# ScalarE's order in the feed-forward inputs, index rotations and Relu in PSUM, the angles in front of the down projection f3_dn

## The reference, cut to what matters

```
h = concat(meta, x)                               # 16 + 256 tokens, 1024 wide
for i in range(2):                                # first model
    h = h + 0.5 * swiglu(rms_norm(h, g[0]), ...)  # f0, f2
    hn = rms_norm(h, g[1])
    h = h + (rwkv7_time_mix(hn, ...) if i == 0 else dsa_attention(hn, ...))
    h = h + 0.5 * swiglu(rms_norm(h, g[2]), ...)  # f1, f3
# swiglu: gate, up = split(h @ w_in); (silu(gate) * up) @ w_out, d_ff 2816
# dsa_attention: an index decides which keys each query sees
qi = partial_rope(qi); ki = partial_rope(ki)      # x * cos + rotated(x) * sin
rel = relu(einsum("bqhd,bkd->bqhk", qi, ki))
score = einsum("bqh,bqhk->bqk", wi, rel)          # then top_k of score
# second model, one layer: two attentions, one with apply_rope on
# ang = positions * inv_freq (cos(ang), sin(ang) computed on the chip), then
hid = square(relu(rms_norm_2(h) @ w_ff1)); h = h + hid @ w_ff2   # 4096 wide
```

## Time and profile before

| what | us |
|---|---|
| median of 3 runs (1659.41 to 1664.03) | 1660.43 |
| profiled execution, its time | 1659.63 |
| its span (first to last instruction) | 1657.8 |
| TensorE busy | 1578.5 |
| GpSimd busy | 1132.7 |
| ScalarE busy | 758.3 |
| VectorE busy | 703.4 |
| mean granted TensorE clock, share of full speed | 0.982 |

### The profile page before, as it was taken

How to read it: one execution, slowest core, us unless ns; L and a number is a source line. 1 busy time by engine, 2 the same in 40 slices (tenths; PEclk the granted TensorE clock), 3 DMA queues, 4 the chain that set the end, 5 groups by cost and what they waited for, 6 DMA issues and landing times.

```text
span 1657.8 us, 40970 instructions
## 1 busy us (share of the span) xinstructions
PE 1578.5 (95%) x16236; PEld 1499.6 (90%) x16236; DVE 703.4 (42%) x1549; ACT 758.3 (46%) x1271; POOL 1132.7 (68%) x835
## 2 busy tenths in 40 slices
PE   6999989899989999999999999999999999989998
PEld 6999989688878999999999986698999978789998
DVE  4332068664556333223331387665321455443300
ACT  5444446743324444454444443554445525545532
POOL 5777858683416777877778773187888954358895
PEclk9999999899999999999999999999999989999999
DMA  6544523310013444455445530164546522225552
GB/s 245 175 171 147 183 100 131 128 65 3 3 53 128 171 172 150 167 203 177 171 145 175 198 137 18 32 234 153 188 153 215 172 102 102 77 92 186 181 203 76
DMA packets 37910, 231.34 MB, mean 140 GB/s; under 512 B 4527, under 2 KB 6680, under 8 KB 16552
## 3 DMA queue, kind: packets, MB, share of 16 engines
q1 hardware_dynamic: 36552, 228.57, 39.2%
q10 hardware_dynamic: 1248, 1.24, 0.2%
HBM read 228.67 MB, written 2.63 MB: 140 GB/s over the span
## 4 chain that ended last, share of the span: by engine, by line
PE 86%; DVE 6%; issue 3%; ACT 2%; POOL 2%; DMA 0%; DVEq 0%; SPq 0%; ACTq 0%; POOLq 0%
PE PS L770 71%; PE PS L769 2%; POOL wlo L724 2%; PE PS L991 1%; PE PS L1368 1%; PE PS L1006 1%; PE PS L998 1%; DVE krot L2326 1%; ACT whi L2492 1%; DVE xl L1702 1%; DMA raw<-w_f_in_in 0%; PE PS L785 0%; PE PS L1030 0%; PE PS L1036 0%; PE PS L1156 0%
## 5 line engine op out<-in xcount | busy, mean ns | idle before, releaser
L724 POOL TENSOR_TENSOR wlo<-raw,whi 128x256 fp32r<-128x256 f32 (+2 forms) x759 | 1086.0, 1462 | 468.8 <-ACT whi L2492 411.8
L770 PE MATMUL PS<-xh,whi 128*128 128x272 f32 (+1 forms) x2336 | 676.5, 290 | 30.2 <-POOL wlo L724 23.9
L770 PE MATMUL PS<-xl,whi 128*128 128x272 f32 (+1 forms) x2336 | 668.6, 286 | 0.0
L770 PE MATMUL PS<-xh,wlo 128*128 128x272 f32 (+1 forms) x2336 | 668.2, 286 | 0.0
L2492 ACT ACTIVATE whi<-raw 128x1024 fp32r<-128x1024 f32 x472 | 449.6, 982 | 259.8 <-PE PS L770 223.2
L770 PEld LDWEIGHTS PS<-xh,whi 128*128 128x128 f32 x2336 | 440.9, 189 | 39.6 <-issue 26.3
L770 PEld LDWEIGHTS PS<-xl,whi 128*128 128x128 f32 x2336 | 442.1, 189 | 0.4
L770 PEld LDWEIGHTS PS<-xh,wlo 128*128 128x128 f32 x2336 | 442.4, 189 | 0.0
L770 PE MATMUL PS<-hid_h,whi 128*128 128x272 f32 (+1 forms) x960 | 274.1, 285 | 4.2 <-POOL wlo L724 4.2
L770 PE MATMUL PS<-hid_h,wlo 128*128 128x272 f32 (+1 forms) x960 | 273.8, 285 | 0.0
L770 PE MATMUL PS<-hid_l,whi 128*128 128x272 f32 (+1 forms) x960 | 272.8, 284 | 0.0
(11 more groups left out here) (381 smaller groups left out, 1624.4 us busy)
## 6 DMA issues: line engine op xcount, KB each, us to landing
raw<-w_f_in_in SPq DMA_DIRECT2D x88, 1024.0 KB, 4.8
raw<-w_f_dn_in SPq DMA_DIRECT2D x64, 704.0 KB, 4.0
raw<-w_b_ff_in SPq DMA_DIRECT2D x32, 1024.0 KB, 4.8
raw<-w_rk_k_in SPq DMA_DIRECT2D x4, 1024.0 KB, 4.9
raw<-w_rk_r_in SPq DMA_DIRECT2D x4, 1024.0 KB, 5.0
raw<-w_rk_v_in SPq DMA_DIRECT2D x4, 1024.0 KB, 4.9
raw<-w_rk_o_in SPq DMA_DIRECT2D x4, 1024.0 KB, 4.8
raw<-w_at_q_in SPq DMA_DIRECT2D x4, 1024.0 KB, 5.0
```

The costliest lines, as they stand in the source:

```text
L724: last = nc.gpsimd.tensor_tensor(wlo[U % SPL][:, piece], raw[U % RAW][:, piece], whi[U % SPL][:, piece].bitcast(F32), ALU.subtract)
L770: mm(out, a, b, start=start and n == 0, stop=stop and n == 2, **kw)
```

## The change

It has five edits, with the same work on TensorE, GpSimd and SyncE's queues.

1. ScalarE in the input projections: after the sigmoid of unit u stands `hi(u + 2)`, then `high(u - 1)`. The last four units are written out.
2. The index rotations: a product `rcos = rstd * cos` is made once. The cosine parts are then made from PSUM with `rcos`, the sine parts in PSUM, and one addition is left. `tailr` no longer marks the group as drained; the second reader of that PSUM group, which uses `rcos`, does.
3. Relu of the index products in PSUM; VectorE reads it there, and TensorE waits for VectorE's additions (`index_added`) before it uses the bank again.
4. The 18 angle instructions in one run behind f3's input projection, ahead of the first addition of `f3_dn`; the two `Sin` behind the first two chunks on ScalarE.
5. In `b_ff1` VectorE takes the norm's sum before it waits for the unit, and ScalarE does `hi(u + 2)` ahead of the squares of unit u.

```diff
-            pe.wait_ge(s_free, G0["at_tail"] + 1)
+            pe.wait_ge(s_tail, 1)
...
-                    pe.wait_ge(s_rl, n - 1)
+                    pe.wait_ge(s_ra, 2 * n - 2)
...
-                        if f == "f3" and i is None:
-                            angle_piece(u)
...
-            v.tensor_tensor(tailr[0:72, :], PS[0:72, bank(G), 0:T], rstd[0:72, 0:T], ALU.mult).then_inc(s_free, 1)
+            v.tensor_tensor(tailr[0:72, :], PS[0:72, bank(G), 0:T], rstd[0:72, 0:T], ALU.mult).then_inc(s_tail, 1)
...
+            def index_cosine(u):
+                U, G = U0["at_qi"] + u, G0["at_qi"] + u
+                dve.wait_ge(s_unit, 2 * (U + 1))
+                x, src = qiT[:, 2 * u:2 * u + 2, :], PS[:, bank(G):bank(G) + 2, 0:SEQ]
+                step.do(v.tensor_tensor(x, src, rstd[:, META:T].unsqueeze(1).broadcast_to([128, 2, SEQ]), ALU.mult))
+                v.tensor_tensor(sqq[:, 2 * u:2 * u + 2, :], src, rcos[:, META:T].unsqueeze(1).broadcast_to([128, 2, SEQ]),
+                                ALU.mult).then_inc(s_free, 1)
+
+            def index_sum(u):
+                dve.wait_ge(s_irot, u + 2)
+                ps = PS[:, 4 + 2 * u:6 + 2 * u, 0:SEQ]
+                step(v.tensor_tensor(ps, ps, cs_a[:, 1:2, META:T].broadcast_to([128, 2, SEQ]), ALU.mult))
+                v.tensor_tensor(qiT[:, 2 * u:2 * u + 2, :], sqq[:, 2 * u:2 * u + 2, :], ps, ALU.add).then_inc(s_iout, 1)
+
+            dve.wait_ge(s_dsc, 48)
+            step.do(v.tensor_tensor(rcos[:, :], rstd[:, :], cs_a[:, 0, :], ALU.mult))
+            step.sync()
+            v.tensor_tensor(rta[0:64, 0, :], PS[0:64, bank(G), 0:T], rcos[0:64, :], ALU.mult).then_inc(s_free, 1)
+            index_cosine(0)
...
+            angle_begin()
+            for n in range(2):
+                if n:
+                    dve.wait_ge(s_ang, 1)
+                angle_turns(n)
+                angle_reduced(n)
+                angle_end(n)
             residual("f3_dn", SEQ, 1, 2, 0.5, "b", VEC["norm_mix"], "b")
...
-                    dve.wait_ge(s_unit, val(2 * (U + 1), i, 8))
                     if u == 0:
                         rms("ff", SEQ)
+                    dve.wait_ge(s_unit, val(2 * (U + 1), i, 8))
...
-                        w = last_width(name, u) if u == us[-1] else UW[name]
-                        hi(U0[name] + u + 1, i, 4, w)
-                        if u == 0:
-                            root(fn, n)
                         act.wait_ge(s_gate, val(hb + u + 1, i, 4))
                         f(sig[:, u % 2, 0:n], PS[:, hbank(u), 0:n], ACT.Sigmoid).then_inc(s_sig, 1)
+                        hi(U0[name] + u + 2, i)
                         if u >= 1:
                             high(u - 1, i)
...
-                if n >= 2:
-                    act.wait_ge(s_ra, 2 * n - 2)
-                f(rel[:, n % 2, :, 0:nk], PS[:, 4 + 2 * (n % 2):6 + 2 * (n % 2), 0:nk], ACT.Relu).then_inc(s_rl, 1)
+                ps = PS[:, 4 + 2 * (n % 2):6 + 2 * (n % 2), 0:nk]
+                f(ps, ps, ACT.Relu).then_inc(s_rl, 1)
...
+            residual("f3_dn", SEQ, 1, 2, "b", "b", beside=sines)
...
-                    hi(U0["b_ff1"] + u + 1, i, 4, 2048)
-                    if u == 0:
-                        root("ff", SEQ)
+                    hi(U0["b_ff1"] + u + 2, i)
                     act.wait_ge(s_free, val(G0["b_ff1"] + u + 1, i, 4))
```

More of the change, by code:

```diff
@@ L2151, in index_scores @@
                     dve.wait_ge(s_ra, 2 * n + e + 1)
-            drain_at("at_qi", 0, qiT[:, 0:2, :], META)
-            dve.wait_ge(s_free, G + 1)
+            def index_cosine(u):
[15 more added lines that the diff above has]
+            index_cosine(0)
+            dve.wait_ge(s_free, G + 2)
             dve.wait_ge(s_irot, 1)
[L2156 to L2159, removed]
+            ps = PS[0:64, 7, 0:T]
+            step(v.tensor_tensor(ps, ps, cs_a[0:64, 1, :], ALU.mult))
+            v.tensor_tensor(kiT[0:64, :], rta[0:64, 0, :], ps, ALU.add).then_inc(s_iout, 1)
             dve.wait_ge(s_rcm, 1)
@@ L2530, in body, with residual @@
                 def body(us, i):
-                    us = list(us)
                     for u in us:
-                        w = last_width(name, u) if u == us[-1] else UW[name]
-                        hi(U0[name] + u + 1, i, 4, w)
-                        if u == 0:
-                            root(fn, n)
                         act.wait_ge(s_gate, val(hb + u + 1, i, 4))
                         f(sig[:, u % 2, 0:n], PS[:, hbank(u), 0:n], ACT.Sigmoid).then_inc(s_sig, 1)
+                        hi(U0[name] + u + 2, i)
                         if u >= 1:
                             high(u - 1, i)
-                turns(step, FC, 4, 0, body, 2)
-                hi(U0[fn + "_dn"] + 1)
+                hi(U0[name] + 1)
+                root(fn, n)
+                body(range(2), None)
+                with step.loop((FC - 6) // 4, 0) as i:
+                    body(range(2, 6), i)
+                body(range(FC - 4, FC), None)
                 high(FC - 1, None)
-            def residual(name, n, w, units, norm, split, done=0):
+            def residual(name, n, w, units, norm, split, done=0, beside=None):
                 per = 4 if w == 2 else 2
@@ L2573, in body @@
                                 after_add(j - 1, i)
+                    if beside and i is None:
+                        beside()
                 turns(step, 8 // w, per, 0, body, 1)
@@ L2831, in _, with sines @@
             swiglu_in("f3")
-            for n in range(2):
-                act.wait_ge(s_ang, n + 1)
-                f(cs_b[:, n, :], cs_b[:, n, :], ACT.Sin).then_inc(s_sin, 1)
-            residual("f3_dn", SEQ, 1, 2, "b", "b")
+            def sines():
+                for n in range(2):
+                    act.wait_ge(s_ang, n + 1)
+                    f(cs_b[:, n, :], cs_b[:, n, :], ACT.Sin).then_inc(s_sin, 1)
+            residual("f3_dn", SEQ, 1, 2, "b", "b", beside=sines)
             def latent(g):
@@ L2948, in ff1 @@
                     f(hid2_h[:, o], act2[:, u % 2, :, :].rearrange("p m n -> p (m n)"), ACT.Square).then_inc(s_hf2, 1)
+            hi(U0["b_ff1"] + 1)
+            root("ff", SEQ)
             ff1(range(4), None)
@@ L2951, in _ @@
                 ff1(range(4, 8), i)
-            for u in range(16):
+            for u in range(1, 16):
                 hi(U0["b_ff2"] + u + 1)
```

29 lines of the change are left out of this document (7 added, 22 removed).

## The result

The changed kernel takes 1652.53 us (median of 8 runs, 1649.81 to 1656.25), the kernel before 1662.66 beside it (8 runs): ratio 0.9942, interval 0.9923 to 0.9961, faster by 10.1 us in the medians and by some 9.6 by the ratio, which takes all runs. The prediction was 1664.3, +3.9. The span of the profiled execution is 1652.3, 5.5 less than before.

A forecast was written before the change was run, and what follows sets the result against it. TensorE, busy 1578.5 of 1657.8 us, was taken as the bound, so its waits and half clock count. -10.5 removed, +7.5 in f3_dn and +6.9 in the index part gave +3.9 on 1660.43: 1664.3 us, range 1652.5 to 1667.5.

The forecast's parts named there:

- I go by the first, since `rcos` meets the very same run without gaps: Index part: `rcos` is shut out until GpSimd's run ends at 954.7, TensorE waits 7.25 us: +6.9.
- rival B: Index part: `rcos` is let in after one GpSimd piece, -2.1 to -2.4 there; total 1655.1 us; chance 0.31.
- f3_dn: Its start: angles, slowed by GpSimd, stop TensorE for 5.8 us, plus 1.7 of clock: +7.5, bounds 0 and 10.5.
- C: Start of f3_dn: the angles hide there, no stall; 1656.8 us, or 1647.6 with `rcos` let in; chance 0.17.
- Rival D: Behind both new waits the clock stays at 0.50 for 5.40 us, costing 2.7 each, not 1.7; 1666.3 us; chance 0.12.
- E: Second units of the down projections: their waits stay despite the change; +4.2 over the forecast, 1668.5 us; chance 0.03.
- What the change removes: TensorE's waits for `wlo` at the down projections' second units, in f3's input projection and in `b_ff1` go: -10.5 us.
- The down starts: Second units of the down projections: `hi` ahead of the last two `hid_h` removes TensorE's waits: -4.2 us.
- f3's input projection: Without the angles there, TensorE's waits of 2.03 and 1.91 us for `wlo` go: -3.9.
- `b_ff1`: Norm's sum half a unit earlier and `hi(u + 2)` ahead of the squares remove TensorE's wait for `wlo`: -2.4 us.
- the new order costs nothing inside the loop: Input projections: `hid_h` is late by one `hi` but read only by the down projection, so no cost.
- Edits at nothing: Relu in PSUM (bounds -0.3 and +0.5) and the two `Sin` with table load on idle ScalarE: taken as 0 us.

The follow-up runs named there:

- rcos_mid: The changed kernel with a 64 x 8 VectorE memset ahead of `rcos`, so that it asks later in a GpSimd piece; ratio to the kernel before 0.994.
- order_only: The kernel before with only ScalarE's new order in the feed-forward input projections; ratio to the kernel before 0.9943 (0.9924 to 0.9962).

## Why the prediction was wrong

**The step that failed** is "I go by the first, since `rcos` meets the very same run without gaps", with its term +6.9. It measured -2.2 from 871 to 956 us, the lower bound of the prediction (-2.1 to -2.4), rival B. Of all products with two SBUF inputs beside a gapless run I had one long row (6.97) and one short (0.95), and explained the difference by the gaps in GpSimd's run. That reading was wrong: `rcos` asked inside a gapless run in eighteen profiles, and each time it was let in at once (14) or after one piece (4).

The trace of before could have told it. It holds 59 VectorE products with two SBUF inputs and 128 to 544 columns that ask during a GpSimd piece of 256 columns with the next piece right behind it. 57 of them were through within 1.25 us, many of them in the middle of runs of 20 such pieces; two were shut out, `kiT` and `krot`. In VectorE's timeline of before:

```profile
249.46 3.72 DVE L1932 SCALAR_TENSOR_TENSOR PS<-xx,vec,hn 128x272 f32<-128x272 f32 x4
254.49 0.98 DVE L1932 SCALAR_TENSOR_TENSOR PS<-xx,vec,hn 128x272 f32<-128x272 f32 x1
```

The rule of the Trainium skill (SBUF — State Buffer, Who interferes with whom), that the loser is blocked while the other's instruction holds the ports, described the four waits of `rcos`: rcos_mid's 0.75 us at 0.28 us into a piece of 0.74 is one. In the other fourteen profiles `rcos` went first although a piece had started 0.04 to 0.07 us before it by the record. It does not describe `krot` (9.5 to 10.3 us over 14 or 15 pieces in a row, in all 16 profiles that have it at its place) and `kiT` in before and order_only (6.97 and 6.98 over 10), which stay unexplained.

**f3_dn** was right in mechanism and nearly in size: 5.36 us of wait and 7.1 in all against 5.8 and 7.5. The burst began at 1217.4 and not at 1224, in a trace that ran 5.9 us ahead of before at that place, four instructions were blocked instead of six, and GpSimd ran dry at 1225.8. So C, which hides the angles, falls. The clock behind it, windows of the changed kernel:

```profile
1235.19:1240.10 4.91, 4.91 (x29) 4.91 (x30) 0.00 (x0) 2.10 (x5) 4.26 (x3) 0.67 0.44 147
```

0.33 x 4.91 = 1.6 us, where 1.7 was taken from the earlier trace rows. Rival D, the whole stretch at 0.50, falls. E falls as well: no wait at the second unit of a down projection is left.

**What the change removes** was right in place and too small in size: -10.5 against -14.3. The down starts gave -6.2 instead of -4.2, f3's input projection -4.8 instead of -3.9, and `b_ff1` -3.3 instead of -2.4. Counting no clock behind the short waits was right, as the window of before behind the wait of 2.03 us shows (clock 1.00):

```profile
1126.08:1131.00 4.92, 4.92 (x41) 4.92 (x42) 4.85 (x3) 1.79 (x2) 4.92 (x3) 1.00 0.24 58
```

But each wait costs some 0.26 us more than its row says: with a wait the matmul behind it starts 0.28 us plus the idle time after the one before, without it 0.12, and the next matmul starts 0.1 late as well. Seven waits make 1.8 of the 3.8 us; the rest are smaller differences that I had left out, 0.6 at f0's start, 0.3 early in f3's input projection, 0.3 late in it and 0.7 in `b_ff1`. That the new order costs nothing inside the loop holds only without the angles: in order_only, where they still stand in f3_in, it loses 1.2 us there. Together with rival B's index part, -14.3 + 7.1 - 2.2 = -9.4. Of the forecast's error of some 13 us the one term of `rcos` is 9.1, some two thirds; the rest is nearly all these sizes.

**Edits at nothing.** Relu in PSUM cost 0.2 us by matched matmuls (one wait of 0.1 us at 982), within the bounds.

The range (1652.5 to 1667.5) holds the measured median by 0.03 us, and that is luck: the forecast was put on 1660.43, and the kernel before then measured 1662.66; 9.6 us under 1660.43 is 1650.8, outside the range. It ended too early because B was given its own sum and no spread: the sizes of B's other terms were uncertain by 4 us too.

## What to carry to other kernels

A long row of VectorE beside GpSimd is one event; before it carries a term of 7 us, look for all rows of its kind, count how many were let in (here 57 of 59), and let the range hold both ends with weight. Independent work moved to "an idle engine" is free only if nothing on the chain stands behind it on that engine: here 18 small instructions in one run cost 7.1 us, and two or three a unit nothing that TensorE's matmuls show. Set two traces against each other matmul by matmul; spans of single profiles differed by 8 us in code that nobody had touched.

## What the hardware showed

`rcos`, a VectorE product with two SBUF inputs, asked 0.06 us after the start of a GpSimd piece, went first, and the piece took 1.09 us instead of 0.73; asked at 0.28 it took 0.75 instead of 0.43 and the next piece 0.94. That is no rule of the moment: the product at 254.49 asked at 0.06 too and waited for the piece (0.98 us in all), and `krot` was passed over by 14 pieces in a row (9.92 us) at one place of this program, in every kernel that had it there, with both operands and both forms tried and asked at 0.05 to 0.08 or at 0.46 to 0.47. `kiT` was passed over by 10 (6.97 us) at another place. Moving `krot`, or giving it one PSUM operand, was enough.
